# Query transposes of a hybrid attention layer: two heads to a TensorE transpose instead of one doubled head

## What is computed

```python
q = apply_rope(rms_norm(q.reshape(B_, S_, NSA_HEADS, dh), q_norm_w), pos)
...
    s_c = jnp.einsum('bgqrd,bcgd->bgqrc', qb, k_c).astype(jnp.float32) * scale
...
    s_s = jnp.einsum('bgqrd,bgqnld->bgqrnl', qb, k_g).astype(jnp.float32) * scale
...
    s_w = jnp.einsum('bgqrd,bkgd->bgqrk', qb, k_wb).astype(jnp.float32) * scale
```

## Time and profile before

| | value |
|---|---|
| median of three runs | 650.41 us (649.8 to 650.52) |
| the profiled execution's own time | 650.0 us |
| its span on the core | 648.2 us |
| TensorE busy | 635.0 us, 98% |
| VectorE busy | 484.9 us, 75% |
| ScalarE busy | 377.9 us, 58% |
| GpSimd busy | 202.5 us, 31% |
| granted TensorE clock | 1.0 of full speed |

### The profile page before, as it was taken

One profiled execution on the slowest core, in us unless ns is written; L12 is line 12 of the kernel. 1 busy time (PEld: TensorE's weight loads), 2 busy tenths in 40 slices (PEclk: granted clock), 3 DMA queues, 4 the chain that ended last, 5 costly groups with the idle time before them and its releaser, 6 DMA issues.

```text
span 648.2 us, 10319 instructions
## 1 busy us (share of the span) xinstructions
PE 635.0 (98%) x3513; PEld 531.9 (82%) x3513; DVE 484.9 (75%) x1153; ACT 377.9 (58%) x872; POOL 202.5 (31%) x220
## 2 busy tenths in 40 slices
PE   9999999999999999999999999998999999999997
PEld 6889998888888888888887887886878877787875
DVE  4955979997745754776788867898887778787853
ACT  6754457564354444556566656678766656665651
POOL 2543304343333323323223212358642221311210
PEclk9999999999999999999999999999999999999999
DMA  8523112102111111101111010133311101101111
GB/s 303 174 57 116 37 30 52 50 32 82 32 50 33 50 33 33 41 27 34 32 34 33 18 33 17 42 106 104 110 48 56 44 33 62 37 33 50 49 34 66
DMA packets 20212, 37.35 MB, mean 58 GB/s; under 512 B 2880, under 2 KB 4288, under 8 KB 20160
## 3 DMA queue, kind: packets, MB, share of 16 engines
q1 hardware_dynamic: 20016, 36.68, 18.3%
q10 hardware_dynamic: 144, 0.00, 0.0%
HBM read 32.48 MB, written 4.19 MB: 57 GB/s over the span
## 4 chain that ended last, share of the span: by engine, by line
PE 84%; DVE 9%; issue 2%; ACT 2%; DMA 1%; POOL 1%; SPq 0%; ACTq 0%; DVEq 0%
PE pf L1464 11%; PE pf L1465 10%; PE pf L1466 10%; PE tp L1778 5%; PE sc L1618 5%; PE sc L1617 4%; PE pj L1464 4%; PE pj L1465 4%; PE pj L1466 4%; PE po L1755 4%; PE po L1756 4%; PE sc L1464 3%; PE sc L1465 3%; PE sc L1466 3%; DVE sc L1371 2%
## 5 line engine op out<-in xcount | busy, mean ns | idle before, releaser
L963 ACT CAST pth<-tp 128x512 fp32r<-128x512 f32 (+1 forms) x148 | 86.9, 587 | 106.3 <-PE tp L1778 105.7
L1371 DVE CUSTOM_DVE_ANT_0 sc<-sc,maskb 128x64 f32<-128x64 f32 (+8 forms) x192 | 103.0, 560 | 44.7 <-PE sc L1618 44.0
L1393 DVE TENSOR_TENSOR ptl<-tp,pth 128x512 fp32r<-128x512 f32 x132 | 90.9, 688 | 23.9 <-ACT pth L963 23.5
L683 POOL TENSOR_SCALAR qp<-qp,precip,gate 128x64 f32<-128x64 f32 x64 | 43.2, 675 | 184.3 <-DVE precip L1361 184.0
L643 POOL TENSOR_TENSOR fl<-fraw,fh 128x512 fp32r<-128x512 f32 x40 | 53.7, 1342 | 97.0 <-ACT fh L808 97.0
L1464 PE MATMUL pf<-hh,fh 128*128 128x512 f32 x200 | 80.3, 402 | 2.8 <-DVE th L1331 1.7
L1465 PE MATMUL pf<-hl,fh 128*128 128x512 f32 x200 | 78.3, 392 | 0.0
L1466 PE MATMUL pf<-hh,fl 128*128 128x512 f32 x200 | 78.1, 391 | 0.0
L634 POOL TENSOR_TENSOR wl<-qp,wh 128x512 fp32r<-128x512 f32 (+1 forms) x33 | 49.4, 1518 | 87.4 <-ACT wh L723 83.7
L1778 PEld LDWEIGHTS tp<-idr,qpr 128*128 128x128 f32 (+1 forms) x592 | 61.7, 137 | 11.8 <-issue 1.8
L1778 PE MATMUL tp<-idr,qpr 128*128 128x128 f32 (+1 forms) x592 | 68.2, 238 | 1.2 <-DVE ptl L1393 0.4
(11 more groups left out here) (259 smaller groups left out, 1550.3 us busy)
## 6 DMA issues: line engine op xcount, KB each, us to landing
fraw<-in_wside SPq DMA_DIRECT2D x40, 256.0 KB, 2.7
qp<-in_wpack SPq DMA_DIRECT2D x28, 256.0 KB, 3.4
xo<-in_x SPq DMA_DIRECT2D x16, 256.0 KB, 2.7
out<-xo SPq DMA_DIRECT2D x16, 256.0 KB, 2.0
wor<-in_wout SPq DMA_DIRECT2D x12, 256.0 KB, 2.8
mixc<-in_xcm SPq DMA_DIRECT2D x4, 512.0 KB, 7.4
xlow<-in_xcm SPq DMA_DIRECT2D x3, 512.0 KB, 6.8
qp<-in_wpack SPq DMA_DIRECT2D x5, 224.0 KB, 2.6
```

The source lines that it names most:

```text
L963: nc.scalar.copy(pth[ptn % 2][0:r, :], tp[tpn % 2][0:r, :]).then_inc(pth_ready, 1)
L1371: return V.tensor_tensor_reduce(row, row, mask, -1.0, -NEG, ALU.add, ALU.min, most)
L1393: V.tensor_tensor(ptl[ptn % 2][:, :], tp[tpn % 2][:, :], pth[ptn % 2][:, :].bitcast(F32), ALU.subtract).then_inc(tp_read, 1)
```

## The change

Two heads lie beside each other in the normalised queries (128 columns), so one transpose of them puts the first head on partitions 0 to 63 and the second on 64 to 127. TensorE now turns two such tiles per unit straight from `qp` instead of four tiles of doubled rows. ScalarE casts the two halves of the bank in two instructions of 64 partitions by 256 columns, both to partitions 0 to 63 of `qh`, waits for its second cast, and copies the whole of `qh` (64 by 512) to partitions 64 to 127. VectorE subtracts in two instructions of 64 by 256; the lower half of `ql`, partitions 64 to 127, is set to zero once ahead of the first unit, so the product of low query and low key is left out. `qh_ready` now counts three per unit, and TensorE's first scores of a unit wait for the third. GpSimd's `copy_queries` and its tile `qd` are gone.

```diff
--- before.py
+++ after.py
@@ -383,9 +383,6 @@
                 with ExitStack() as f:
                     fraw = [sb(f"fraw{s}", [P, 512], F32, f) for s in range(2)]
                 wor = [None, None] + [sb(f"wor{s}", [P, 512], F32, d) for s in (2, 3)]
-                with ExitStack() as f:
-                    qdr = sb("qdr", [P, GH, 2, HD], F32R, f)
-                qd = sb("qd", [P, GH, 2, HD], F32, d)
                 qh = sb("qh", [P, GH, P], F32R, d)
                 ql = sb("ql", [P, GH, P], F32R, d)
                 pth = [sb(f"pth{s}", [P, 512], F32R, d) for s in range(2)]
@@ -443,7 +440,7 @@
         conv_first, conv_done = sem("conv_first"), sem("conv_done")
         wor_in = [sem(f"wor_in{s}") for s in range(4)]
         woh_ready, wol_ready = sem("woh_ready"), sem("wol_ready")
-        qd_ready, qh_ready, kend_ready = sem("qd_ready"), sem("qh_ready"), sem("kend_ready")
+        qh_ready, kend_ready = sem("qh_ready"), sem("kend_ready")
         s_done, max_ready, exp_done = sem("s_done"), sem("max_ready"), sem("exp_done")
         recip_ready, factor_ready = sem("recip_ready"), sem("factor_ready")
         p_act, p_dve, cmp_scaled = sem("p_act"), sem("p_dve"), sem("cmp_scaled")
@@ -643,17 +640,6 @@
                 nc.gpsimd.tensor_tensor(fl[h % 3][:, :], fraw[h % 2][:, :], fh[h % 3][:, :].bitcast(F32), ALU.subtract)\
                     .then_inc(fl_ready, 1)
 
-            def copy_queries(u):
-
-                i, g = UNITS[u]
-                if u >= 1:
-                    pool.wait_ge(q_normed, 2)
-                    pool.wait_ge(qh_ready, u)
-                src = qn[:, i, g * 256:(g + 1) * 256].rearrange("p (h d) -> p h d", h=GH)
-                for twice in range(2):
-                    ins = nc.gpsimd.tensor_copy(qd[:, :, twice, :], src)
-                ins.then_inc(qd_ready, 1)
-
             def copy_last_keys(u):
 
                 i, g = UNITS[u]
@@ -664,8 +650,6 @@
             for e in range(NE):
                 entry_weights(e)
             pool.wait_ge(hid_done, 2)
-            pool.wait_ge(q_normed, 1)
-            copy_queries(0)
             for h in range(2):
                 half_lo(h)
             pool.wait_ge(kt_ready, 9)
@@ -682,9 +666,6 @@
                     p = cmp_probs(i, s % 4)
                     nc.gpsimd.tensor_scalar(p, p, precip[:, s % 4, 1:2], gate_of(s, 0), ALU.mult, ALU.mult)\
                         .then_inc(cmp_scaled, 1)
-                u = unit_at(k, -5)
-                if u:
-                    copy_queries(u)
                 u = unit_at(k, -6)
                 if u is not None and u >= 2:
                     copy_last_keys(u)
@@ -856,7 +837,12 @@
                 act.wait_ge(tp_done, tpn + 1)
                 if u >= 1:
                     act.wait_ge(s_done, 8 * u)
-                nc.scalar.copy(qh[:, :, :], tp[tpn % 2][:, :].rearrange("p (h q) -> p h q", h=GH)).then_inc(qh_ready, 1)
+                pairs = qh[:, :, :].rearrange("p (j e) q -> p j e q", e=2)
+                for e in range(2):
+                    src = tp[tpn % 2][e * HD:(e + 1) * HD, 0:2 * P].rearrange("p (j q) -> p j q", j=2)
+                    nc.scalar.copy(pairs[0:HD, :, e, :], src).then_inc(qh_ready, 1)
+                act.wait_ge(qh_ready, 3 * u + 2)
+                nc.scalar.copy(qh[HD:P, :, :], qh[0:HD, :, :].bitcast(F32)).then_inc(qh_ready, 1)
                 tpn += 1
 
             def keys_hi(first, n0, b):
@@ -1208,9 +1194,12 @@
 
             def queries(u):
                 nonlocal tpn
-                dve.wait_ge(qh_ready, u + 1)
-                V.tensor_tensor(ql[:, :, :], tp[tpn % 2][:, :].rearrange("p (h q) -> p h q", h=GH),
-                                qh[:, :, :].bitcast(F32), ALU.subtract).then_inc(tp_read, 1)
+                pairs_h, pairs_l = (v[:, :, :].rearrange("p (j e) q -> p j e q", e=2) for v in (qh, ql))
+                for e in range(2):
+                    dve.wait_ge(qh_ready, 3 * u + e + 1)
+                    src = tp[tpn % 2][e * HD:(e + 1) * HD, 0:2 * P].rearrange("p (j q) -> p j q", j=2)
+                    ins = V.tensor_tensor(pairs_l[0:HD, :, e, :], src, pairs_h[0:HD, :, e, :].bitcast(F32), ALU.subtract)
+                ins.then_inc(tp_read, 1)
                 tpn += 1
 
             def keys_lo(first, n0, b):
@@ -1401,6 +1390,8 @@
                 dve.wait_ge(xo_in[c % 2], 16 * (c // 2 + 1))
                 V.tensor_tensor(xo[c % 2][:, :], side_bank(NF + c), xo[c % 2][:, :], ALU.add).then_inc(out_ready, 1)
 
+            dve.wait_ge(qh_ready, 1)
+            V.memset(ql[HD:P, :, :].bitcast(F32), 0.0)
             queries(0)
             side(0)
             dve.wait_ge(masks_in, 16)
@@ -1602,12 +1593,13 @@
 
             def queries(u):
                 nonlocal tpn
-                pe.wait_ge(qd_ready, u + 1)
+                pe.wait_ge(q_normed, 1 if u == 0 else 2)
                 if tpn >= 2:
                     pe.wait_ge(tp_read, tpn - 1)
-                for h in range(GH):
-                    ins = nc.tensor.transpose(tp[tpn % 2][:, h * P:(h + 1) * P].bitcast(F32R),
-                                              qdr[:, h, :, :].rearrange("p u d -> p (u d)"), idr[:, :])
+                i, g = UNITS[u]
+                for j in range(2):
+                    o = (8 + i) * 512 + (2 * g + j) * P
+                    ins = nc.tensor.transpose(tp[tpn % 2][:, j * P:(j + 1) * P].bitcast(F32R), qpr[:, o:o + P], idr[:, :])
                 ins.then_inc(tp_done, 1)
                 tpn += 1
                 q_tp[u] = tpn
@@ -1621,6 +1613,7 @@
                 w, h = divmod(k, 4)
                 i, g = UNITS[w // 2]
                 if h == 0 and w % 2 == 0:
+                    pe.wait_ge(qh_ready, 3 * (w // 2) + 3)
                     pe.wait_ge(tp_read, q_tp[w // 2])
                 if h == 0 and w % 2 == 1:
                     pe.wait_ge(kend_ready, w // 2 + 1)
```

## The result

The changed kernel takes 654.27 us (median of five runs, 653.79 to 654.44) against 650.41 before; the ratio of the runs is 1.0065, 95% interval 1.0054 to 1.0077: slower, by some 4.2 us by the ratio and 3.9 by the two medians. The profiled execution took 654.37, with a span of 652.6.

A forecast was written before the change was run, and what follows sets the result against it. TensorE was taken as the bound, busy 635.0 of 648.2 us, with waits where ScalarE's delay reaches it. 4.8 - 1.3 - 0.5 = +3.0 us on 650.0, plus 0.4 for the median, gave 653.4 us, range 650.2 to 656.0.

The forecast's parts named there:

- the 0.4 that was added for the median of before: Whole kernel: the median shown, 650.41, lies 0.4 above the profiled execution's 650.0, so 653.0 became 653.4 us.
- ScalarE's price: ScalarE's query casts: three hold it 1.45 us instead of 0.48, making exponentials and high parts 0.8 us later.
- The other price that was worked out: ScalarE's three casts by the Trainium skill: 1.26 us, a delay of 0.62 instead of 0.8.
- The six places: Behind units 6, 9, 11, 13, 14 and 15 ScalarE's delay reaches TensorE: 6 x 0.8 = 4.8 us.
- VectorE's price: VectorE's two query subtractions, 0.42 us each: maxima come about 0.3 earlier, nothing else, since the low parts wait for pth.
- TensorE's saving: Query transposes on TensorE: two fewer give 0.16 us per unit, 2.5 over 16 units if no wait takes it back.
- the list of units that keep it: Units 0 to 5, 7 and 10 keep TensorE's 0.16 us each, 1.3 us in all.
- GpSimd's copies: GpSimd's two removed copies per unit: worth 0 to 0.9 us, taken as 0.5, at one place near 445 us.
- The rival in which effects cancel: Only three or four of six places pass on 0.58 us: 2.0 against 1.8 of gains, within 0.2% of 650.4; chance 0.2.
- That of more places: Slack behind units 7, 8, 10 and 12 used up too, some 0.5 us each: +6.0, 656.4 us; chance 0.1.

The follow-up runs named there:

- the kernel with one more: The changed kernel with a third VectorE subtraction of 64 by 256 ahead of the second one's release, into an unread tile: 654.82 us against 650.0, ratio 1.0076.
- the late-copy version: The changed kernel with ScalarE's third copy behind the next step's first high parts instead of ahead of the exponentials: 650.08 us against 650.0, ratio 1.0003.

## Why the prediction was right

The forecast was 653.4 with slower at 0.67; it came out at 654.27, inside the range and by the likeliest mechanism. The distance of 0.9 flatters it: the sum was +3.0 us against 4.2 measured, and the 0.4 that was added for the median of before was scatter, since every later median of that kernel is 650.0 to 650.07.

**ScalarE's price: right.** 1.45 was forecast from the first cast to the exponentials, and it is 522.25 - 520.82 = 1.43. The casts take 0.37 each and 0.62, the third starts 0.03 behind the second's end and the exponentials 0.02 behind the third's. The other price that was worked out, by the Trainium skill (ScalarE: Activation LUTs, What ACT_TABLE_LOAD costs) with an overlap of 93 ns between neighbours, gave 1.26, and 1.9 for the sum; the shifted copy has no overlap here, and the row of a shifted copy was the better guide.

**The six places: right.** They are the units named, 4.67 us against 4.8. That it is ScalarE's queue is shown from both sides, by adding its work to the kernel before (+5.1 us) and by moving one copy in the changed one (back to 650.1; the steps fell by 0.64 to 0.74 at five of the six, and by 0.32 at unit 11, where the moved copy is waited for itself). What the prediction had not said is that at units 6 and 9 the late exponentials stop the next scores first; it changes no sum.

**VectorE's price: right at the six, not at units 5, 7 and 10.** The maxima start 0.10 sooner at unit 13, not 0.3: the two subtractions run 0.43 apart without overlapping, and the first waited for the first cast. At the six places it makes no difference, as the kernel with one more shows. The prediction put it at nothing everywhere; where VectorE comes late to the queries, the split holds it 0.88 instead of 0.60, and the maxima came 0.3 later. In the changed kernel that is no more than ScalarE's delay in units 5 and 7 (in unit 7 pth ends at 3.33, and ptl starts at 3.38); in unit 10 VectorE is the later of the two (pth ends at 3.44, ptl starts at 3.62), and in the late-copy version it is what delays ptl in unit 7.

**TensorE's saving: right in size, short in the sum.** 0.13 to 0.26 a unit in units 0 to 4, 0.18 in the mean, taken as 0.16. What was wrong is the list of units that keep it. Units 5 and 7 were to save 0.16 each and lost 0.06 and 0.16; units 8 and 12 were to give nothing and lost 0.10 and 0.44; unit 10 was to save 0.16 and has +0.24 with GpSimd's copies back. There are two reasons. The 0.31 from the transposes to the turn was read at unit 13 and taken for every unit; in units 5, 7 and 10 it was 0.6 in the trace of before, so the turn already waited for an earlier ptl, as was seen for unit 12 alone, and two transposes less only lengthen that wait. And I had held the first ptl behind the queries against TensorE's next use of it and stopped there; behind units 7 and 12 TensorE waits for what GpSimd does behind a scaling, further down the same chain, which starts 0.30 and 0.77 later.

Units 5, 7, 8 and 12 together cost 1.1 us more than the sum had, and unit 10 another 0.4; against that stand 0.2 more from the copies, 0.1 less at the six places and 0.1 more saved in units 0 to 4. That leaves about 1.05 of the 1.40 by which the span's change was missed, and the rest is the 0.35 ahead of unit 0.

**GpSimd's copies: right mechanism, 0.7 instead of 0.5.** Where the Trainium skill (SBUF — State Buffer, SBUF: two separate sides) says that the engines lock each other out for a whole instruction, the two traces agree. VectorE's instruction takes 0.69 by itself, and in both it ends 0.55 after GpSimd's first weight subtraction does (449.46 to 450.01 with the copies, 448.56 to 449.11 without), however long ago it started; GpSimd's second subtraction takes 1.7 instead of 1.3 there.

The rival in which effects cancel fell because all six places passed the delay on. That of more places named units 7, 8, 10 and 12 and was right about the units, but they lost 0.1 to 0.44 each, not 0.5. Its sum, 4.8 + 2.0 - 0.8, doesn't follow from its own terms either: six units' saving and the copies come to 1.5, so it is +5.3, or 655.7.

## What to carry to other kernels

Look behind the instruction that is changed on its own engine, not at it: of the three instructions on ScalarE, the third costs 4 us more ahead of the next high parts than behind them. TensorE, 98% busy, lost more to 0.8 us in front of somebody else's high parts than two transposes a unit gave back. Where two engines' arms meet within 0.03 us, a delay of either should count in full; it was measured for ScalarE's arm, while VectorE's was only tried with slack in front of it (0.42 more left no trace at the six places). Put what isn't needed soon behind what is, and look up its first reader: here the next unit's scores, which did wait for the moved copy at units 6, 8, 9 and 11. Read a price at every place before it is multiplied: the 0.31 of one unit was 0.5 to 0.8 in six others. And when following slack, go on to the next two or three readers down the chain, since a first reader with room to spare doesn't mean that the delay ends there.

## What the hardware showed beyond that

On ScalarE, a copy from one half of the partitions to the other neither overlaps its predecessor nor its successor (0.62 long, followed after 0.02), while a cast that stays on its partitions is followed 0.1 ahead of its end by the exponentials, which use the same ones. The first of the two half-width casts stays on partitions 0 to 63, but its successor reads the other half, and it isn't overlapped either (0.76 for the two, 0.37 each). On VectorE the two subtractions of 64 partitions, the second of which reads the other half, run end to end too, 0.42 each and 0.43 apart; when the third subtraction stood between, reading and writing the same halves as its successor, that successor started 0.35 behind it (522.11 to 522.46). So in these rows the overlap is missing where an instruction starts on another half of the partitions than the one ahead, and not because it moves data between halves; the last pair is the only one of its kind here, and on ScalarE no such pair was run. A wait of ScalarE on its own last instruction costs next to nothing: the third copy starts 0.03 behind the second cast, the exponentials, which have no such wait, 0.02 behind the copy.
